# Gate and up products of four feed-forward layers: the split input's two parts in one 512-column matmul, summed afterwards

## The reference, cut to what matters

```python
def swiglu(h, w_gate, w_up, w_down):
    return (jax.nn.silu(h @ w_gate) * (h @ w_up)) @ w_down

mod = (c_act @ ada_w[layer] + ada_b[layer]).reshape(bsz, N_SUB, 3, D_MODEL)[:, :, :, None, :]
x = x + HALF_STEP * (1.0 + mod[:, 0, 2]) * swiglu(h, ffn_w_gate[layer, 0], ffn_w_up[layer, 0], ffn_w_down[layer, 0])
```

## Time and profile before

| | us |
|---|---|
| median of 3 runs | 2375.23 (2374.82 to 2380.11) |
| the profiled execution, its time | 2379.18 |
| the profiled execution, its span | 2377.1 |
| TensorE busy | 2235.8 |
| VectorE busy | 1714.2 |
| ScalarE busy | 1177.6 |
| mean granted TensorE clock | 0.962 of full |

### The profile page before, as it was taken

How to read it: one execution, slowest core, us unless ns; L and a number is a source line. 1 busy time by engine, 2 the same in 40 slices (tenths; PEclk the granted TensorE clock), 3 DMA queues, 4 the chain that set the end, 5 groups by cost and what they waited for, 6 DMA issues and landing times.

```text
span 2377.1 us, 33631 instructions
## 1 busy us (share of the span) xinstructions
PE 2235.8 (94%) x13648; PEld 1977.1 (83%) x13648; DVE 1714.2 (72%) x2145; ACT 1177.6 (50%) x1392; POOL 234.8 (10%) x183
## 2 busy tenths in 40 slices
PE   7789999998789999997999989899999999988998
PEld 7768888888578888886998988699989988867997
DVE  5566679995666678997877786777777766576554
ACT  3553356883553356785334673443343344534333
POOL 5200312312000301310000011000000020000000
PEclk9889999998889999998999999999999999999999
DMA  9127779994118779995886323388678834305652
GB/s 252 54 94 301 257 255 331 362 353 187 55 41 299 246 254 328 343 370 193 303 268 229 144 72 135 133 285 289 223 238 290 277 130 146 125 1 201 198 178 71
DMA packets 241450, 505.55 MB, mean 213 GB/s; under 512 B 10383, under 2 KB 104529, under 8 KB 241296
## 3 DMA queue, kind: packets, MB, share of 16 engines
q1 hardware_dynamic: 216144, 417.84, 50.3%
q10 hardware_dynamic: 21600, 77.09, 9.1%
q0 software_dynamic: 3552, 8.47, 1.5%
HBM read 502.31 MB, written 1.05 MB: 212 GB/s over the span
## 4 chain that ended last, share of the span: by engine, by line
PE 61%; DVE 9%; ACT 2%; issue 1%; DMA 0%; ACTq 0%; DVEq 0%
PE PS L1075 21%; PE PS L1091 10%; PE PS L921 7%; PE PS L1175 5%; PE PS L879 4%; PE PS L1274 2%; PE PS L1294 2%; DVE WGL L2324 2%; PE PS L1184 1%; PE PS L1338 1%; DVE AR L2327 1%; PE PS L1553 1%; DVE XN L2324 1%; PE PS L1370 1%; DVE AR L2324 1%
## 5 line engine op out<-in xcount | busy, mean ns | idle before, releaser
L2324 DVE TENSOR_TENSOR WGL<-ring,WGH 128x2048 fp32r<-128x2048 f32 (+1 forms) x291 | 601.2, 2074 | 231.0 <-ACT WGH L1761 116.0
L1075 PE MATMUL PS<-XTB,WGH 128*128 128x256 f32 x2816 | 516.3, 285 | 5.3 <-DVE XTB L2324 4.9
L1075 PEld LDWEIGHTS PS<-XTB,WGH 128*128 128x128 f32 x2816 | 447.5, 193 | 15.9 <-issue 8.1
L1075 PE MATMUL PS<-XTB,WGL 128*128 128x256 f32 x1408 | 400.0, 284 | 0.0
L1075 PEld LDWEIGHTS PS<-XTB,WGL 128*128 128x128 f32 x1408 | 271.6, 193 | 0.0
L2324 DVE TENSOR_TENSOR WDL<-ring,WDH 128x1024 fp32r<-128x1024 f32 (+1 forms) x136 | 217.0, 1595 | 32.1 <-ACT WDH L1921 22.8
L1921 ACT ACTIVATE WGH<-ring 128x2048 fp32r<-128x2048 f32 x96 | 183.3, 1914 | 112.7 <-PE PS L1175 39.4
L1761 ACT ACTIVATE WGH<-ring 128x1024 fp32r<-128x1024 f32 (+2 forms) x107 | 145.1, 1361 | 179.8 <-PE PS L879 59.8
L921 PE MATMUL PS<-XTB,WGH 128*128 128x256 f32 x1088 | 206.4, 291 | 12.7 <-DVE WGL L2324 9.8
L1964 ACT ACTIVATE XN<-PS 128x256 f32<-128x256 f32 x88 | 33.8, 384 | 353.7 <-PE PS L1075 326.9
L921 PEld LDWEIGHTS PS<-XTB,WGH 128*128 128x128 f32 x1088 | 173.3, 195 | 23.8 <-DVE WGL L2324 11.6
(11 more groups left out here) (513 smaller groups left out, 4468.3 us busy)
## 6 DMA issues: line engine op xcount, KB each, us to landing
FA<-in_ada_w ACTq DMA_DIRECT2D x144, 512.0 KB, 6.2
ring<-in_moe_w_up SPq DMA_DIRECT2D x64, 1024.0 KB, 7.2
ring<-in_moe_w_gate SPq DMA_DIRECT2D x64, 1024.0 KB, 7.9
ring<-in_moe_w_down SPq DMA_DIRECT2D x64, 1024.0 KB, 7.4
ring<-in_ffn_w_gate SPq DMA_DIRECT2D x44, 1024.0 KB, 5.5
ring<-in_ffn_w_up SPq DMA_DIRECT2D x44, 1024.0 KB, 9.5
ring<-in_ffn_w_down SPq DMA_DIRECT2D x44, 1024.0 KB, 7.3
ring<-in_hyb_w_in SPq DMA_DIRECT2D x10, 1152.0 KB, 7.2
```

Source lines behind the costliest of these rows:

```text
L1075: ins = mm(PS[:, 4 + b, m * T:(m + 1) * T], w_[:, b, w], x_[:, k, :], start=k == 0 and q == 0, stop=k == KD - 1 and q == 2)
L2324: return V.tensor_tensor(out_, x_, y_, op)
```

## The change

In `gate_up`, high weights by high x and high weights by low x become one matmul of 512 columns: `XTB[:, :, k, :]` is both parts of slice k, and the output is a whole bank, the two partial sums side by side. The low weights by high x stay a matmul of 256 columns, added to the first half. A chunk has 32 matmuls in place of 48, with 12,288 columns as before. Gate and up of a chunk now take two banks, 4 and 5 or 6 and 7. The two halves of each bank are summed behind TensorE: ScalarE copies the second halves (2 x 256 columns) to SBUF (`GUL`, semaphore `gu_low`), VectorE adds the first halves from PSUM (`GUS`, `gu_sum`), ScalarE takes the silu from SBUF, and VectorE's product has both operands in SBUF.

Banks 6 and 7 are no longer free: `gate_row` of the feed-forward stages goes to banks 2 and 3, so down(0) waits for ScalarE's copy of it. `sums_by_token` goes into the two banks that hidden(j) has emptied, waits for hidden(j), and VectorE's reduction of it moves ahead in the chunk behind: before its wait for silu rather than behind `WGL`. gate_up(6), gate_up(11) and gate_up(16) wait for that reduction's result (`mod_out`). Nothing changes in the other stages.

The diff, cut to its core:

```diff
-        SG = XNF[:, 0:512].rearrange("p (b t) -> p b t", b=2)
-        HR = XNF[:, 512:1024].rearrange("p (b t) -> p b t", b=2)
+        GUL = XNF[:, 0:1024].rearrange("p (b m t) -> p b m t", b=2, m=2)
+        GUS = XNF[:, 1024:2048].rearrange("p (b m t) -> p b m t", b=2, m=2)
...
                     b = j % 2
+                    if turn is not None and j % 5 == 1 and 6 <= j <= 16:
+                        pe.wait_ge(S("mod_out"), turn + j // 5)
                     for m in range(2):
+                        both = PS[:, 4 + 2 * b + m, :].rearrange("p (i t) -> p i t", i=2)
                         for k in range(KD):
...
-                            for q, (w_, x_) in enumerate(((WGH, XTH), (WGH, XTL), (WGL, XTH))):
-                                ins = mm(PS[:, 4 + b, m * T:(m + 1) * T], w_[:, b, w], x_[:, k, :],
-                                         start=k == 0 and q == 0, stop=k == KD - 1 and q == 2)
+                            if k < KD - 1:
+                                mm(both, WGH[:, b, w], XTB[:, :, k, :], start=k == 0, stop=False,
+                                   skip_group_check=True)
+                            ins = mm(both[:, 0, :], WGL[:, b, w], XTH[:, k, :], start=False, stop=False,
+                                     skip_group_check=True)
+                            if k == KD - 1:
+                                ins = mm(both, WGH[:, b, w], XTB[:, :, k, :], start=False, stop=True,
+                                         skip_group_check=True)
                     ins.then_inc(S("gate_up"), 1)
                 def ready(j):
+                    if j == 0:
+                        pe.wait_ge(S("row"), r.v2 + 1)
                     pe.wait_ge(S("lo_dn"), r.cb + j + 1)
...
                     if turn is not None and j % 5 == 4 and j < 15:
-                        if j == 4:
-                            pe.wait_ge(S("row"), r.v2 + 1)
-                        sums_by_token(turn + j // 5)
+                        pe.wait_ge(S("hidden"), r.cb + j + 1)
+                        sums_by_token(turn + j // 5, 4 + 2 * (j % 2))
...
(ScalarE, hidden_layer)
-                    f(SG[:, j % 2, :], PS[:, 4 + j % 2, 0:T], ACT.Silu).then_inc(S("silu"), 1)
+                    b = j % 2
+                    f(GUL[:, b, :, :], PS[:, 4 + 2 * b:6 + 2 * b, T:2 * T], ACT.Copy).then_inc(S("gu_low"), 1)
+                    act.wait_ge(S("gu_sum"), r.cb + j + 1)
+                    f(GUL[:, b, 0, :], GUS[:, b, 0, :], ACT.Silu).then_inc(S("silu"), 1)
...
(VectorE, hidden)
+                    dve.wait_ge(S("gu_low"), r.cb + j + 1)
+                    tt(GUS[:, b, :, :], PS[:, 4 + 2 * b:6 + 2 * b, 0:T], GUL[:, b, :, :], ALU.add).then_inc(S("gu_sum"), 1)
+                    if turn is not None and j % 5 == 0 and 5 <= j <= 15:
+                        done, o = turn + j // 5 - 1, 4 + 2 * ((j - 1) % 2)
+                        dve.wait_ge(S("mod_ps"), done + 1)
+                        c(V.tensor_reduce(M8[:, 0:AW // P], PS[:, o:o + 2, :].rearrange("p b (m n) -> p (b m) n", n=P),
+                                          AX.X, ALU.add))
+                        mod_out(done, M8[:, 0:AW // P])
                     dve.wait_ge(S("silu"), r.cb + j + 1)
...
-                    then(tt(HR[:, b, :], SG[:, b, :], PS[:, 4 + b, T:2 * T]))
+                    then(tt(GUL[:, b, 1, :], GUL[:, b, 0, :], GUS[:, b, 1, :]))
```

More of the change, by code:

```diff
@@ L1134, in mod_sums, with sums_by_token @@
                 ins.then_inc(S("mod_ps"), 1)
-            def sums_by_token(turn):
+            def sums_by_token(turn, bank):
                 pe.wait_ge(S("mod_acc"), TURN * (turn + 1))
@@ L1140, in sums_by_token @@
                 for m in range(AW // P):
-                    ins = nc.tensor.transpose(PS[:, 6 + m // 4, m % 4 * P:(m % 4 + 1) * P], ADC[:, m * P:(m + 1) * P], ID)
+                    ins = nc.tensor.transpose(PS[:, bank + m // 4, m % 4 * P:(m % 4 + 1) * P], ADC[:, m * P:(m + 1) * P], ID)
                 ins.then_inc(S("mod_ps"), 1)
@@ L1147, in last_sums, with gate_row @@
                     mod_sums(LAST_TURN[r.name], PS[:, 6, 0:AW // P])
-            def gate_row(r):
+            def gate_row(r, bank=6):
                 pe.wait_ge(S("diag"), r.v2 + 1)
                 for j in range(2):
-                    ins = mm(PS[:, 6 + j, :], ONES[:, 0:P],
+                    ins = mm(PS[:, bank + j, :], ONES[:, 0:P],
                              DG[:, 4 * j:4 * j + 4, :].rearrange("p k d -> p (k d)"), start=True, stop=True)
@@ L1448, in ffn @@
                 trn(r.u, XN)
-                hidden_layer(r, lambda: gate_row(r))
+                hidden_layer(r, lambda: gate_row(r, 2))
             def mod(r):
@@ L1775, in gate_row_out @@
                 act.wait_ge(S("row_ps"), r.v2 + 1)
-                f(ROWB[:, 0, :], PS[:, 6:8, :].rearrange("p j n -> p (j n)"), ACT.Copy).then_inc(S("row"), 1)
+                b = 2 if r.items else 6
+                f(ROWB[:, 0, :], PS[:, b:b + 2, :].rearrange("p j n -> p (j n)"), ACT.Copy).then_inc(S("row"), 1)
             def attention(r, units):
@@ L2721, in hidden @@
                         dve.wait_ge(S("w_used"), r.wb + j - 1)
-                    then(tt(HR[:, b, :], SG[:, b, :], PS[:, 4 + b, T:2 * T]))
-                    then(V.tensor_copy(HTH[:, b, 0:T], HR[:, b, :]))
-                    tt(HTL[:, b, 0:T], HR[:, b, :], HTH[:, b, 0:T].bitcast(F32), ALU.subtract).then_inc(S("hidden"), 1)
+                    then(tt(GUL[:, b, 1, :], GUL[:, b, 0, :], GUS[:, b, 1, :]))
+                    then(V.tensor_copy(HTH[:, b, 0:T], GUL[:, b, 1, :]))
+                    tt(HTL[:, b, 0:T], GUL[:, b, 1, :], HTH[:, b, 0:T].bitcast(F32), ALU.subtract).then_inc(S("hidden"), 1)
                 after = AFTER[r.name] if r.name in AFTER else None
@@ L2735, in hidden_layer @@
                         split_low(r, j + 2, True)
[L2736 to L2741, removed]
                     if q is not None:
```

## The result

| | us | ratio to before, 95% interval |
|---|---|---|
| before, median of 7 runs | 2376.11 (2374.04 to 2380.11) | |
| the change, median of 7 runs | 2383.94 (2379.97 to 2385.92) | 1.0029 (1.0020 to 1.0039) |
| forecast | 2378.3 (2366 to 2387) | |

By the ratio the change costs 6.9 us (4.8 to 9.3), just under the 0.3% that the prediction takes for no change; its interval lies wholly above 1. The profiled execution took 2383.27 us, its span is 2381.4.

A forecast was written before the change was run, and what follows sets the result against it. TensorE's matmuls were taken to bound settled chunks. Matmuls -14.4, stage ends +5.5, starts of three stages +9.0 and ada_w landings +3.0 sum to +3.1 us: 2378.3 us, range 2366 to 2387.

The forecast's parts named there:

- The end of a stage: Last down of each of four stages: copy and add become 1.37 us of new waiting, +5.5 us in all.
- The late chunk of VectorE: Start of ffn00, ffn01, ffn10: a chunk where VectorE is behind takes it 8.86 us, against TensorE's 8.33.
- gate_up(6): In ffn00, ffn01, ffn10 it waits 2.3 us for the reduction's mod_out, part of +3.0 us per stage.
- Settled chunks, gate row, ffn11: Settled chunks cover the 1.37 us; the gate row's copy costs nothing; ffn11 loses only at its end.
- the matmuls: Gate and up in 88 chunks: 5.58 us a chunk for 5.75, -14.4 us in all.
- Starts and landings together: ffn00, ffn01, ffn10: +9.0 us for VectorE's lag at the starts and +3 us for late ada_w slices.
- 10.6 ns saved per pair: Gate and up: one 512-column matmul costs 229 ns, two of 256 columns 239.6.
- the landings: VectorE's waits for ada_w slices reach TensorE: 1.0 us in each of three stages, +3 us, between 0 and 10.
- rival 4: TensorE's clock falls to 0.50 for 4 us behind the new gaps: +2 us a stage, 2384 us; chance 0.04.
- Rival 1: VectorE's lag doesn't reach TensorE, only stage ends are lost: -8.9, 2366 us; chance 0.19.
- Rival 2: ada_w slices land too late and VectorE bounds three stages: +10, 2385 us; chance 0.19.
- Rival 3: The split operand costs what merging saves, gate_up stays at 5.75 us: +13, 2388 us; chance 0.08.

The follow-up runs named there:

- tail_old: The change with three 256-column matmuls and silu straight from PSUM again in the last chunk of all four feed-forward stages: 2376.53 us, ratio 1.0003 to before.
- early_old: The change with the old products in chunks 0 to 5 of ffn00, ffn01 and ffn10: 2375.4 us, ratio 0.9994 to before.
- old_chunks_0_to_3: The change with the old products in chunks 0 to 3 of ffn00, ffn01, ffn10 and the last chunk of all four stages: 2369.05 us, ratio 0.9966.
- no_sums: The change's matmuls without copy and add, high weights by low x left out of the result: 2362.7 us, ratio 0.9943 to before.
- both_old_again: Second run of the change with old products in chunks 0 to 5 of ffn00, ffn01, ffn10 and the last chunk of all four stages: 2367.28 us, ratio 0.9954.
- two_of_256: The change with each 512-column matmul split again into two of 256, copy and add kept: 2392.06 us, ratio 1.0061 to before.
- grouped: The change with the eight 512-column matmuls of each of gate and up first, the eight 256-column ones behind: 2384.17 us, ratio 1.0028 to before.
- contiguous: The change with the 512 moving columns in one run, from two neighbouring high-part slices, low x left out: 2385.23 us, ratio 1.0031 to before.
- reduce_first: The change with VectorE's reduction and bias ahead of the add in chunks 5, 10 and 15: 2382.34 us, ratio 1.0026 to before.

## Why the prediction came out as it did

**Right, and confirmed by undoing it.** *The end of a stage*: forecast 1.37 us in four stages, measured 1.38 or 1.39 of waiting, and tail_old takes it away. *The late chunk of VectorE*: forecast 8.86, measured 8.84 and 8.85. *gate_up(6)*: forecast a wait of 2.3 us, measured 2.2; early_old removes it, and old_chunks_0_to_3 and no_sums show that it is the lag and not the place of the reduction alone. *Settled chunks, gate row, ffn11*: no added cost beside the matmuls and the end; gate_up(11) and gate_up(16) start at once in the change's trace; ffn11 was to be shorter by 2.3 and is by 1.6. Starts and landings together were put at 12.0 us (9.0 + 3.0) and came to 13.2 by the ledger, 10.8 by early_old.

**Mis-sized: the matmuls.** The step "10.6 ns saved per pair" should have read 7.5 (5.63 us for 5.75 over 16 pairs). It put together two spacings that each length has among its own kind; in turn they cost 352 ns, not 349. With the down's 0.02 us the term is -12.3 by the trace and -13.5 +- 3.6 by no_sums, for -14.4 forecast. I had named the mixing of lengths as a gap in the rows but no price for it. The Trainium skill (TensorE: Matmul & The Clock Gate, "Wait — 56ns, not 53.3ns?") puts the fixed cost of a matmul at the full clock at about 2.5 ns, by which gate_up would take an estimated 5.71 us. The traces don't agree: 5.63 us.

**Half right: the landings.** "1.0 us per stage" was an allowance. VectorE's waits for slices came to 9.4 us in 14 places over the span, no more than in the earlier trace rows. One of 1.22 us reached TensorE in ffn00, one of 0.23 stood in ffn01, and ffn10 had none ahead of chunk 5. So the cost sat in one stage and wasn't spread over three. Ahead of the sums TensorE lost 1.8, 1.2 and 0.7 us beyond a settled chunk, lag and landings together, against 1.7 forecast.

**Held too unlikely: rival 4.** The clock did fall behind the gap of gate_up(6), in one of three stages of the change's trace, for 1.5 us. I gave the rival 0.04 and all three stages; it is neither all nor none. The change costs about twice the +3.1 that was forecast, and +3.1 lies below the measured interval of 4.8 to 9.3. Of the 3.5 us between the forecast and the ledger 2.1 are missing from the matmuls and 1.5 are that one fall; the rest nearly cancels (gate_up(0) of ffn10 +0.6, ends +0.2, the other costs of the starts 0.9 less than the 12.0 forecast).

Rival 1 is out, since the lag reaches TensorE in all three stages. Rival 2, landings that bind three stages, isn't in the change's trace, where VectorE waited for slices no more than before; but late slices can use up the 0.7 us by which the prediction had the reductions of chunks 10 and 15 covered, as both_old_again shows. Rival 3, the pair no cheaper, is out by no_sums and two_of_256.

## What to carry to other kernels

When work moves from the engine that bounds to engines that don't, count it at the places where nothing lies over it: the last chunk of each stage, and chunks in which the helping engine is already late. There the old form can be kept for a few chunks, and here 22 of 88 chunks in the old form turned +6.9 us into -10.5. Take a matmul's price from a sequence of the same lengths in the same order, and reckon with a low clock after a bare gap of about 2 us in a dense stream.

## What the runs showed of the hardware

**Price of a matmul.** With fp32r operands and a weight load each, 512 and 256 columns in turn take 352 ns a pair; in groups of eight, as grouped has them, eight of 512 take 1.81 or 1.84 us, eight of 256 take 0.96 or 0.95, and a pair is 5.56 / 16 = 348 ns. A moving operand in two runs costs what one in one run does (5.63 us for 16 pairs in the change and in contiguous).

**The clock behind a gap.** Where TensorE had stood for 1.89 to 2.20 us in the feed-forward stages (16 places in the traces of the change, tail_old, contiguous, grouped, two_of_256 and reduce_first), the granted clock was at the 1.2 GHz level right behind it in 10, and gate_up(6) took 7.2 to 7.3 us for 5.7. It differs from stage to stage and between kernels with the same gap: in the change in ffn10, in tail_old in ffn00. Behind the three gaps of 1.58 to 1.60 at gate_up(6), the one of 1.44, and the waits of 1.4 at the ends of the stages, no stretch of matmuls was lengthened so. What decides between falling and not was not tried.
